# A hybrid decoder block on one core: the opening of the first FFN in two passes, the conditioning row turned on TensorE, and a finer wait in the tails

## The reference, cut to what matters

```
ada = (silu(c) @ w_ada + b_ada)              # 9 vectors of 2048: sh1 sc1 gt1 sh2 sc2 gt2 sh3 sc3 gt3
h = rmsnorm(x, g_ffn1) * (1 + sc1) + sh1
x = x + 0.5 * gt1 * ((silu(h @ w1_gate) * (h @ w1_up)) @ w1_down)        # FF = 5632
h = rmsnorm(x, g_mix) * (1 + sc2) + sh2
x = x + gt2 * (token_mix(h @ w_in) @ w_out)  # 8 dilated attention heads, 8 retention heads
h = rmsnorm(x, g_ffn2) * (1 + sc3) + sh3
x = x + 0.5 * gt3 * ((silu(h @ w2_gate) * (h @ w2_up)) @ w2_down)
out = rmsnorm(x, g_final)
```

## Time and profile before

| | |
|---|---|
| three runs | 1975.89 to 1976.83 us, median 1976.55 |
| the profiled execution | 1977.3 us, of which the span from first to last instruction is 1975.5 |
| PE busy | 1894.3 us, 96% of the span |
| DVE busy | 1308.2 us, 66% |
| ACT busy | 847.4 us, 43% |
| DMA | 507.65 MB, mean 257 GB/s |
| granted clock of PE, mean | 0.984 of full speed |

### The profile page before, as it was taken

The page is one execution under the profiler, slowest core; times in us unless marked ns, Lnnn a source line. Parts: engine busy times, 40 slices in busy tenths (PEclk is TensorE's granted clock), DMA queues, the critical chain, the costliest instruction groups (busy, mean ns, idle before and its releaser), DMA issues. The chain is left out here.

```text
span 1975.5 us, 21076 instructions
## 1 busy us (share of the span) xinstructions
PE 1894.3 (96%) x8376; PEld 1551.8 (79%) x8376; DVE 1308.2 (66%) x1346; ACT 847.4 (43%) x964; POOL 0.2 (0%) x4
## 2 busy tenths in 40 slices
PE   4768999999999999999999999999999999999997
PEld 3557888888888888788887787888888888888886
DVE  7776787878777878676664676666655555544454
ACT  5324444433444434544544544544443334444443
POOL 0000000000000000000000000000000000000000
PEclk9879999999999999999999999999999999999999
DMA  9996888888888888488444464777765555556553
GB/s 404 370 352 235 317 336 340 312 345 301 344 333 332 327 315 338 153 336 302 157 164 150 157 251 154 260 276 286 277 211 190 185 189 193 190 187 210 189 191 118
DMA packets 117889, 507.65 MB, mean 257 GB/s; under 512 B 13600, under 2 KB 13856, under 8 KB 98336
## 3 DMA queue, kind: packets, MB, share of 16 engines
q1 hardware_dynamic: 117792, 506.31, 69.6%
HBM read 504.14 MB, written 2.12 MB: 256 GB/s over the span
## 5 line engine op out<-in xcount | busy, mean ns | idle before, releaser
L742 DVE TENSOR_TENSOR w_lo<-w_raw,w_hi 128x1024 fp32r<-128x1024 f32 x652 | 796.2, 1224 | 553.7 <-ACT w_hi L564 553.2
L564 ACT CAST w_hi<-w_raw 128x1024 fp32r<-128x1024 f32 x652 | 683.8, 1050 | 1047.1 <-PE banks L996 1024.1
L994 PE MATMUL banks<-w_hi,x_split 128*128 128x512 f32 x1776 | 707.7, 398 | 44.1 <-DVE x_split L857 44.1
L996 PE MATMUL banks<-w_hi,x_split 128*128 128x512 f32 x1776 | 697.9, 393 | 0.0
L995 PE MATMUL banks<-w_lo,x_split 128*128 128x512 f32 x1776 | 697.8, 393 | 0.0
L994 PEld LDWEIGHTS banks<-w_hi,x_split 128*128 128x128 f32 x1776 | 337.7, 190 | 116.1 <-issue 42.8
L996 PEld LDWEIGHTS banks<-w_hi,x_split 128*128 128x128 f32 x1776 | 337.4, 190 | 72.5
L995 PEld LDWEIGHTS banks<-w_lo,x_split 128*128 128x128 f32 x1776 | 338.0, 190 | 68.4
L994 PE MATMUL banks<-w_hi,hidden 128*128 128x512 f32 x704 | 279.6, 397 | 4.9 <-DVE w_lo L742 4.9
L995 PE MATMUL banks<-w_lo,hidden 128*128 128x512 f32 x704 | 279.1, 396 | 0.0
L996 PE MATMUL banks<-w_hi,hidden 128*128 128x512 f32 x704 | 278.9, 396 | 0.0
(11 more groups left out here) (122 smaller groups left out, 586.1 us busy)
## 6 DMA issues: line engine op xcount, KB each, us to landing
w_raw<-w_chunks SPq DMA_DIRECT2D x656, 512.0 KB, 4.1
ada_raw<-w_ada_tiles SPq DMA_DIRECT2D x112, 1024.0 KB, 5.7
ada_early<-w_ada_tiles SPq DMA_DIRECT2D x32, 1024.0 KB, 6.9
gate_row<-gate_rows SPq DMA_DIRECT2D x3, 1024.0 KB, 5.3
residual<-x_t SPq DMA_DIRECT2D x2, 1024.0 KB, 6.8
out_t<-residual SPq DMA_DIRECT2D x4, 512.0 KB, 3.1
table<-tables SPq DMA_DIRECT2D x1, 1664.0 KB, 7.4
cond_row<-c_t SPq DMA_DIRECT2D x1, 1024.0 KB, 4.5
```

The costliest lines, as they stand in the source:

```text
L564: nc.scalar.copy(w_parts(c)[0], raw[:, c % RING, :]).then_inc(hi_ready, 1)
L742: nc.vector.tensor_tensor(lo, raw[:, c % RING, :], hi.bitcast(F32), ALU.subtract).then_inc(lo_ready, 1)
L994: nc.tensor.matmul(o, x_hi, hi, start=(first and k == k0), stop=False, skip_group_check=True)
L996: ins = nc.tensor.matmul(o, x_lo, hi, start=False, stop=(last and k == k0 + KC - 1), skip_group_check=True)
```

## The change

Four things are done.

1. **The opening in two passes.** The four groups that run side by side first are now gate 2, up 2, gate 3, up 3 of the FFN ("parted"). They run over slices 0 to 3 only (16 chunks); their partial sums are copied by ACT from the banks to SBUF ("set aside", in the unused `gate_row` and the part of `table` that is not loaded yet). Then gate 0, up 0, gate 1, up 1 ("whole") run side by side over all eight slices (32 chunks). Then the parted groups run over slices 4 to 7 (16 chunks), and DVE adds what was set aside (gate_sum, and in product). The 32 early ada tiles are spread over chunks 0 to 41: four a slice up to slice 3, then 16 over 26 chunks. The later ada tiles begin at chunk 44 instead of 32 and end at the same one. The number of chunks, matmuls and ada tiles is as before.
2. **A slice's order.** DVE and SP now go ada, ada, ada, w, w, ada, scale, w, low, w; ACT does modulate_first before the w_hi of the slice's last chunk.
3. **The start.** c is loaded as 128 x 16; ACT takes silu, PE turns its 16 columns, spread over 128 columns each, into four banks, and ACT copies these to `cond_row`. The loads are ordered c, identity, first half of x, bias, gains, second half of x.
4. **The tails.** The wait on the last chunk's w_lo ahead of the tail becomes a wait for each chunk as it is used.

The core of the diff:

```diff
+PART = 4
+    start, middle = FIRST * PART, FIRST * (PART + SLICES)
     for i in range(FIRST):
-        add((GATE, UP)[i % 2], i, SLICES, i, FIRST)
-    at = FIRST * SLICES
+        add((GATE, UP)[i % 2], i, 0, 0, chunks=range(start + i, middle, FIRST))
+    at = 2 * FIRST * SLICES
+    for i in range(FIRST):
+        add((GATE, UP)[i % 2], i, 0, 0, chunks=[*range(i, start, FIRST), *range(middle + i, at, FIRST)])
...
+WHOLE, PARTED, LATER = GROUPS[:FIRST], GROUPS[FIRST:2 * FIRST], GROUPS[2 * FIRST:]
+OPEN_END = 2 * FIRST * SLICES
+ADA_FROM = FIRST * (PART + SLICES) - RING
...
-ADA_PACE = ((FIRST * SLICES, 0), (MARKS["in"] - 8, 82), (MARKS["in"] + 6, 82), (MARKS["in"] + 33, 91),
+ADA_PACE = ((ADA_FROM, 0), (MARKS["in"] - 8, 82), (MARKS["in"] + 6, 82), (MARKS["in"] + 33, 91),
...
+            if g in PARTED:
+                put(e, ("gate_sum", g.n))
...
-            turn = e + (2 if g.n != 1 else 5)
+            turn = e + 2 if g.n >= FIRST else OPEN_END + 2 + 2 * g.n
...
     order = [("ada", i) for i in range(4)] + [("scale", 0), ("w", 0), ("low", 0)]
-    order += [("w", 1), ("ada", 4), ("w", 2), ("ada", 5), ("w", 3)]
-    for s in range(1, SLICES):
+    order += [("w", 1), ("ada", 4), ("w", 2), ("ada", 5), ("w", 3), ("ada", 6), ("w", 4), ("w", 5), ("ada", 7), ("scale", 1),
+              ("w", 6), ("low", 1), ("w", 7)]
+    for s in range(2, PART):
         i = 4 * s
-        if s > 1:
-            order += [("ada", i), ("ada", i + 1)]
-        order += [("w", i), ("w", i + 1), ("ada", i + 2), ("w", i + 2), ("ada", i + 3), ("scale", s), ("w", i + 3), ("low", s)]
+        order += [("ada", i), ("ada", i + 1), ("ada", i + 2), ("w", i), ("w", i + 1), ("ada", i + 3), ("scale", s),
+                  ("w", i + 2), ("low", s), ("w", i + 3)]
+    i, start, end = 4 * PART, FIRST * PART, ADA_FROM
+    pending = None
+    for c in range(start, end):
+        order.append(("w", c))
+        if pending is not None:
+            order.append(("low", pending))
+            pending = None
+        if i < 4 * SLICES and (c - start) * 16 // 26 >= i - 4 * PART:
+            order.append(("ada", i))
+            i += 1
+            if i % 4 == 0:
+                pending = i // 4 - 1
+                order.append(("scale", pending))
...
-            sp.dma_start(c_row[:, :], c_in.to_broadcast([P, D])).then_inc(c_in_sem, 16)
+            sp.dma_start(c_col[:, :], c_in).then_inc(c_in_sem, 16)
+            sp.dma_start(tab[:, 0:EARLY_COLS], table_in_hbm[:, 0:EARLY_COLS]).then_inc(ident_in, 16)
+            sp.dma_start(xs[:, 0, :], x_in[:, 0, :]).then_inc(x_in_sem[0], 16)
             sp.dma_start(ada[:, :], b_ada).then_inc(const_in, 16)
             sp.dma_start(gain[:, :, :], gains_in).then_inc(const_in, 16)
...
+            sp.dma_start(xs[:, 1, :], x_in[:, 1, :]).then_inc(x_in_sem[1], 16)
...
+            def set_group_aside(g):
+                act.wait_ge(w_free, g.chunks[PART - 1] + 1)
+                nc.scalar.copy(both(aside(g)), ps[:, 2 * g.side:2 * g.side + 2, :]).then_inc(set_aside, 1)
...
+                if g in PARTED:
+                    act.wait_ge(gate_summed, b - PARTED[0].n + 1)
+                    nc.scalar.activation(aside(g), aside(g), ACT.Silu).then_inc(silu_ready, 1)
+                    return
...
+            act.wait_ge(c_turned, 1)
+            nc.scalar.copy(c_row[:, :], ps[:, 4:8, :].rearrange("p b n -> p (b n)")).then_inc(c_ready, 1)
...
+            def gate_sum(b):
+                g = group(GATE, b)
+                dve.wait_ge(w_free, g.last + 1)
+                nc.vector.tensor_tensor(both(aside(g)), ps[:, 2 * g.side:2 * g.side + 2, :], both(aside(g)),
+                                        ALU.add).then_inc(gate_summed, 1)
...
             def tail(g, n):
 
-                pe.wait_ge(lo_ready, g.last + 1)
                 for t in range(2):
                     for i in range(g.count - TAIL, g.count):
+                        if t == 0:
+                            pe.wait_ge(lo_ready, g.chunks[i] + 1)
...
+            for k in range(DT):
+                ins = nc.tensor.transpose(ps[:, 4 + k // 4, k % 4 * P:k % 4 * P + P], c_col[:, k:k + 1].to_broadcast([P, P]), ident)
+            ins.then_inc(c_turned, 1)
             for j in range(8):
                 turn_x(j)
-            for s in range(SLICES):
-                for g in GROUPS[:FIRST]:
-                    chunk(g, s)
+            for groups, slices in ((PARTED, range(PART)), (WHOLE, range(SLICES)), (PARTED, range(PART, SLICES))):
+                for i in slices:
+                    for g in groups:
+                        chunk(g, i)
```

More of the change, by code:

```diff
@@ L41, with __init__ @@
 class Group:
[L45 to L48, removed]
+    def __init__(self, kind, n, side, chunks, ahead=None, tile0=0, column=0):
+        self.kind, self.n, self.side, self.chunks, self.count = kind, n, side, list(chunks), len(chunks)
+        self.first, self.last = self.chunks[0], self.chunks[-1]
+        self.ahead, self.tile0, self.column = ahead, tile0, column
 GATE, UP, DOWN, IN, OUT = "gate", "up", "down", "in", "out"
@@ L57, in plan, with add @@
     numbers = {GATE: 0, UP: 0, DOWN: 0, IN: 0, OUT: 0}
-    def add(kind, side, count, first, step=1, tile0=0, column=0):
-        g = Group(kind, numbers[kind], side, first, count, step, held.get(side), tile0, column)
+    def add(kind, side, count, first, tile0=0, column=0, chunks=None):
+        g = Group(kind, numbers[kind], side, chunks or range(first, first + count), held.get(side), tile0, column)
         numbers[kind] += 1
@@ L431, in hid_bank, with aside, group, hid_source @@
         def hid_bank(b):
-            return 6 if b == 1 else 4
+            return 6 if b in (1, 3) else 4
+        def aside(g):
+            at = (g.n - PARTED[0].n) * 2 * GW
+            if g.kind == GATE:
+                return gate_row[:, at:at + 2 * GW]
+            return tab[:, EARLY_COLS + at:EARLY_COLS + at + 2 * GW]
+        def group(kind, n):
+            return next(g for g in GROUPS if g.kind == kind and g.n == n)
+        def hid_source(b):
+            g = group(GATE, b)
+            return aside(g) if g in PARTED else hid_buf(b)[:, :]
+        def both(buf):
+            return buf.rearrange("p (b n) -> p b n", b=2)
         def scaled(q):
@@ L532, in _ @@
                 late_tile(ADA_EARLY + i)
-            for c in range(FIRST * SLICES, CHUNKS):
+            for c in range(ADA_FROM, CHUNKS):
                 w_chunk(c)
@@ L718, in _ @@
             w_hi(3)
[L719 to L723, removed]
+            pending = None
+            for kind, n in OPENING:
+                if kind == "scale" and n > 0:
+                    pending = n
+                elif kind == "w" and n >= FIRST:
+                    w_hi(n)
+                    if pending is not None:
+                        modulate_first(pending)
+                        pending = None
+                    if FIRST * PART <= n < FIRST * PART + FIRST:
+                        set_group_aside(PARTED[n - FIRST * PART])
+            for c in range(ADA_FROM - RING, CHUNKS):
                 if c + RING < CHUNKS:
@@ L975, in _ @@
                     low_first(n)
-            for c in range(FIRST * SLICES - RING, CHUNKS):
+            for c in range(ADA_FROM - RING, CHUNKS):
                 for name, n in SCHEDULE.get(c, ()):
@@ L1019, in turn_hid @@
                 pe.wait_ge(hid_f32, b + 1)
-                if b < 2:
-                    pe.wait_ge(silu_ready if b == 0 else hid_f32, 2)
-                else:
-                    pe.wait_ge(hid_ready, b)
-                h, turned = hid_buf(b), by_tile(hid_bank(b), NT)
+                if b == 0:
+                    pe.wait_ge(gate_summed, 2)
+                elif b == 1:
+                    pe.wait_ge(hid_f32, FIRST)
+                else:
+                    pe.wait_ge(hid_ready, b - 1 if b < FIRST else b)
+                h, turned = hid_source(b), by_tile(hid_bank(b), NT)
                 for n in range(NT):
@@ L1131, in operand @@
             def operand(g, i):
-                if g.kind in (GATE, UP) and g.n < 2:
+                if g.kind in (GATE, UP) and g.n < FIRST:
                     pe.wait_ge(mod_ready, i + 1)
@@ L1147, in chunk @@
             def chunk(g, i):
-                c = g.first + g.step * i
-                if i == 0:
-                    if g.ahead is None:
-                        pe.wait_ge(xt_kept, 4 * (g.side + 1) // 2)
-                    else:
-                        banks_free(g.ahead)
+                c = g.chunks[i]
+                begins = i == 0 or g in PARTED and i == PART
+                if g in WHOLE and begins:
+                    pe.wait_ge(set_aside, g.side + 1)
+                elif g in PARTED and i == 0:
+                    pe.wait_ge(xt_kept, 2 * g.side + 2)
+                elif begins:
+                    banks_free(g.ahead)
                 pe.wait_ge(lo_ready, c + 1)
```

(4 more changed lines are left out.)

51 lines of the change are left out of this document (31 added, 20 removed).

## The result

The changed kernel takes **1925.35 us** (median of 4, 1925.08 to 1925.92) against 1976.69 for the kernel before in the same comparison (4 runs): ratio 0.9739, 95% interval 0.9723 to 0.9756. That is 51.3 us; the forecast was 1923.7, in a range of 1918 to 1940. The profiled execution took 1925.92 us with a span of 1924.1, which is 51.4 less than the span before.

The account below looks back on a forecast made before the run. PE, busy 96% of the span, was taken as the bound. Opening 40.8 plus tails 13.0 less 1.0 for DMA gave 52.8 us off, so 1923.7 us against a median of 1976.55, range 1918 to 1940.

Parts of the forecast that it names:

- The start: Kernel's start: x's second half lands at 8.95 us, moving all of the opening 1.9 us earlier, bounds 0 and 2.8.
- Pass one: Slices 0 to 3: DVE, never held up by PE, sets a period of 15.66 us a slice.
- The last slice: Slice 3, end of pass one: PE starts at 74.7 us and needs 13.23 us, ending the sixteenth chunk at 87.9.
- rival 5: Opening: shorter PE gaps keep the clock high, last slice 10.9 us, start at its bound, no DMA cost: 1919.5 us; chance 0.05.
- Passes two and three: The 48 chunks after pass one: PE runs without a wait, 130.6 us, DVE still about 2.9 us ahead at chunk 43.
- The 1.0 us charged for DMA: Pass two, chunks 16 to 41: 30.4 MB at 424 GB/s need 71.7 us, 1.0 us more than PE's time.
- The tails: Three tails: a w_lo wait per chunk recovers waiting and low clock, 4.35 us each, gain 13.0 us, lower bound 7.3.
- DMA (1937 us): Passes one and two: DMA at 374 GB/s bounds them, 14.1 us less the 1.0 charged, 1937 us; chance 0.14.
- the very signs that I had named for it: Named evidence of a DMA bound: w_hi waiting for DMA in 90 to 160 us, and DMA engines' high busy share.
- Old pace (1933): Pass one: w_hi, held by PE, still stops DVE; slices take 18.7 us, 9.2 us lost, 1933 us; chance 0.08.
- Tails (1937): Three tails: PE meets the same waits a step later, the 13.0 us is not gained, 1937 us; chance 0.08.
- Slower by the clock (2000): Pass two: short waits at each chunk keep PE at 1.2 GHz, 76.8 us more, 2000 us; chance 0.03.

Follow-up runs that it names:

- start_undone: The changed kernel with c loaded as before, as a 1 MB row ahead of x, without the turning on TensorE: 1926.83 us.
- the two experiments: The finer tail wait alone in the kernel before: 1964.8 us against 1976.51; the old tail wait put back in the changed kernel: 1937.38 us.
- tail_undone: The changed kernel with the old single wait for w_lo put back ahead of each tail: 1937.38 us.
- part3: The changed kernel with pass one over three slices instead of four, two ada tiles ahead of pass two and 18 over 26 chunks: 1923.11 us.
- order_undone: The changed kernel with the old order inside the slices of pass one, two passes kept: 1932.24 us.
- squeezed: The changed kernel with the 16 ada tiles of pass two spread over 20 chunks instead of 26: 1931.96 us.
- order_alone: The kernel before with only the new order inside a slice, one pass over eight slices: 1959.68 us against 1976.51.

## Why the prediction was right, step by step

**The start, 1.9 us forecast.** PE's first matmul came at 25.48 instead of 26.46, 1.0 us. c was much faster than thought (landed at 2.34, turned from 3.75 on), but that was not the critical one: the second half of x landed at 9.83, not 8.95. The term was over-sized; the means over the runs give 1.1 us.

**Pass one, 15.66 us a slice forecast.** DVE's timeline of the kernel after:

```profile
43.47 0.69 DVE L932 TENSOR_TENSOR x_split<-scratch,x_split 128x512 fp32r<-128x512 f32 x1 [0.72 <-ACT x_split L689]
...
59.52 0.69 DVE L932 TENSOR_TENSOR x_split<-scratch,x_split 128x512 fp32r<-128x512 f32 x1 [0.72 <-ACT x_split L689]
60.47 1.23 DVE L808 TENSOR_TENSOR w_lo<-w_raw,w_hi 128x1024 fp32r<-128x1024 f32 x1 [0.26 <-ACT w_hi L613]
...
64.53 2.35 DVE L820 CUSTOM_DVE_ANT_0 scratch<-ada_early,cond_row,ada 128x2048 bf16<-128x2048 f32 x1 [0.57 <-DVE ada L820]
...
76.00 0.69 DVE L932 TENSOR_TENSOR x_split<-scratch,x_split 128x512 fp32r<-128x512 f32 x1 [0.72 <-ACT x_split L689]
```

DVE is the bound, as said, and PE is out of its loop; but low_first to the next w_lo takes 0.95 us and not 0.61, since ACT makes that w_hi only after modulating. That is a wait that the change adds, and I had read over it: I took the step from the old order, where the w_hi was done before. With it the period is 16.05. The slice behind 59.52 had 0.4 more, ahead of an ada tile, the fourteenth. It is not that tile's load: the same pause of 0.56 or 0.57 us stands ahead of the same tile in all fourteen traces, in the kernel before and with half the load of that tile too. What it is stays open. Low_first of slice 3 was forecast for 73.8 and came at 76.00: 0.9 of it from the start and the rest from these steps.

**The last slice, 13.23 us forecast.** 152.1 - 149.6 + 10.9 = 13.4. The granted clock was low in each of the four slices (0.77, 0.89, 0.85, 0.81); that PE's gap was shorter now (3.7 us at slice 3) didn't help, so rival 5 fell as a forecast of this kernel's time. What it had in mind does occur: slice 2 of start_undone ran at 0.98. What the clock costs in slice 3 is shown by the zero-adding matmuls, 2.4 us against this trace, and 1.4 to 2.5 over five traces.

**Passes two and three, no wait forecast.** PE had none from 76.84 to the first turn_hid. DVE's last w_lo of the pass ended at 161.0 and PE came to that chunk at 90.3 + 27 x 2.72 = 163.7, a lead of 2.7 where I had 2.9. This was luck in part: I counted 0.8 us for a mod_scale with low_first and it is 1.6, but my stepwise listing had the longer wait in it. The 1.0 us charged for DMA was not paid. In chunks 60 to 69, too, the listing held: w_lo of chunk 67 ended at 229.0 and PE came to it at 229.8.

**The tails, 13.0 us forecast.** 12.9 by the account of spans, 11.7 and 12.0 by the medians of the two experiments. The size held for this trace, but the step from one tail to three assumed that the low clock follows each wait; in tail_undone it followed only two. This term came out of one reading: the wait in the profile is 2.4 us, but the next matmuls stood 0.43 us apart.

**Rivals.** DMA (1937 us): fell. From 90 to 160 us w_hi waited for DMA 10 times for 19.6 us in all (21 times and 37.3 us up to 240), and the engines' share was 1.0, the very signs that I had named for it, but PE waited for nothing, since DVE had its own queue to work through. The loads were halved in part3 only, not in the changed kernel: there, with 266 instead of 425 GB/s, low_first kept their places. So the sign was badly chosen: a wait of ACT for DMA is not a wait of DVE. The Trainium skill's page "DMA: Bandwidth & Descriptors" (Specifications) gives a core about 358 GB/s of HBM; this trace has 402 over 69.5 us and 425 over 18.8, so the page's figure did not bind here. Old pace (1933): fell, 16.05 against 18.7; order_undone, which has the old order, paid 6.9 us for it where the rival had 9.2. Tails (1937): fell. Slower by the clock (2000): fell; PE's clock was full all through pass two, and in the squeezed kernel, with real waits there, it fell to 0.93 for 10 us and came back, at 6.6 us in all.

The sum: 0.9 too much was expected of the start, 1.2 of pass one, 0.2 of the last slice and 0.1 of the tails, and the 1.0 of DMA was not paid: 1.4 us, the difference between the 52.8 forecast and the 51.4 of the spans.

## What to carry to other kernels

When two engines share a loop through a ring, write down what stands behind the waiting instruction in the same queue: here two long, independent steps stood behind a step that waited for PE, and moving them ahead of it gave 17 us without any other change. A short wait of PE can cost its low clock as well, so a wait of 2.45 us was worth 4.3 us in seven of nine cases (before, tail_undone, order_alone) and 2.6 in two: look at more than one trace before you price it; and a wait at the head of a group for its last part is easily made finer. Before believing that a saturated queue is the bound, take half its work away: here that moved the end by 0.7 us, while filling the busiest engine's 0.7 us waits with other work gave 2 us.

## What the runs showed of the hardware

A load of 128 x 16 floats landed 1.6 us after its issue began (0.73 to 2.34) ahead of the large loads, where small loads behind a large one had taken 3.6 to 4.0. With fourteen 128x512 bf16 matmuls that add zero in the idle stretch ahead of slice 3 (3.72 us without them), the slice ran at 2.4 GHz: the following 55 chunks took 149.7 us against 152.1. After a wait of only 2.45 us seven or eight matmuls stood 0.43 us apart, at 1.2 GHz, having been preceded by a few at the full rate; but after the same wait in tail_undone's first tail none did, and the slices behind waits of 2.75 us (start_undone) and 3.21 us (changed kernel) had granted clocks of 0.98 and 0.85. So one kernel's cost of the low clock varied by 1 to 2 us at one place from execution to execution. And 425 GB/s over 18.8 us and 402 over 69.5 us were moved into one core with no loss on DVE: its w_lo took 1.22 us as at 266 GB/s.
